# Softmax division moved behind the weighted sum, layer norm by tokens

## The reference, cut to what matters

```python
# branch A, 8 heads of 64: attention over the keys that an indexer selected
logits = where(selected, q @ k.T * HEAD_DIM**-0.5 + bias, NEG)
p = softmax(logits)                     # exp(l - max) / sum over the keys
attn = p @ v
# branch B, 512 channels: causal depthwise convolution c, then
c = (c - mean) * rsqrt(var + EPS) * g + b    # LayerNorm over the 512 channels
c = silu(c)
```

## Time and profile before

| | us |
|---|---|
| median of 3 runs (1861.46 to 1861.98) | 1861.76 |
| the profiled execution, its own time | 1863.46 |
| span of its trace | 1861.6 |
| PE busy in the span | 1763.3 |
| DVE busy | 1217.5 |
| ACT busy | 764.4 |
| POOL busy | 382.3 |

### The profile page before, as it was taken

How to read it: one execution, slowest core, us unless ns; L and a number is a source line. 1 busy time by engine, 2 the same in 40 slices (tenths; PEclk the granted TensorE clock), 3 DMA queues, 4 the chain that set the end, 5 groups by cost and what they waited for, 6 DMA issues and landing times.

```text
span 1861.6 us, 30230 instructions
## 1 busy us (share of the span) xinstructions
PE 1763.3 (95%) x11736; PEld 1587.2 (85%) x11736; DVE 1217.5 (65%) x2161; ACT 764.4 (41%) x1609; POOL 382.3 (21%) x457
## 2 busy tenths in 40 slices
PE   7978999999899987988999999999999999999999
PEld 6936999999889854667988789999999999888877
DVE  4279998999799666766453577555565654444443
ACT  4376666221565267655122443322222222333332
POOL 4104332331784122330000001111111112000000
PEclk9999999999999998998999999999999999999999
DMA  6411112221212424774332213222222222657574
GB/s 200 72 53 46 35 40 104 96 100 47 84 49 69 157 59 153 255 259 183 140 119 75 84 52 94 72 71 72 71 77 72 77 72 94 214 172 239 176 238 153
DMA packets 92881, 209.22 MB, mean 112 GB/s; under 512 B 13334, under 2 KB 32694, under 8 KB 92484
## 3 DMA queue, kind: packets, MB, share of 16 engines
q1 hardware_dynamic: 86555, 193.26, 32.4%
q10 hardware_dynamic: 6192, 14.16, 1.9%
HBM read 167.77 MB, written 39.58 MB: 111 GB/s over the span
## 4 chain that ended last, share of the span: by engine, by line
PE 40%; issue 14%; DVE 3%; ACT 2%; DMA 1%; POOL 1%; SPq 1%; POOLq 0%; DVEq 0%; ACTq 0%
PE ps L831 12%; PE ps L833 12%; PE ps L832 12%; DVE buf L1687 1%; DMA buf<-f_scr 1%; PE ps L1083 1%; PE ps L1060 1%; DVE buf L1893 1%; ACT buf L1493 1%; DVE buf L2259 1%; PE ps L1102 0%; PE ps L1117 0%; PE ps L1073 0%; SPq L799 0%; PE ps L1089 0%
## 5 line engine op out<-in xcount | busy, mean ns | idle before, releaser
L833 PE MATMUL ps<-buf,buf 128*128 128x288 f32 (+3 forms) x2660 | 877.3, 330 | 0.0
L832 PE MATMUL ps<-buf,buf 128*128 128x288 f32 (+3 forms) x2660 | 877.2, 330 | 0.0
L831 PE MATMUL ps<-buf,buf 128*128 128x288 f32 (+3 forms) x2484 | 828.5, 334 | 19.9 <-DVE buf L1687 10.7
L833 PEld LDWEIGHTS ps<-buf,buf 128*128 128x128 f32 (+1 forms) x2660 | 501.2, 188 | 24.4
L832 PEld LDWEIGHTS ps<-buf,buf 128*128 128x128 f32 (+1 forms) x2660 | 501.5, 189 | 23.5
L831 PEld LDWEIGHTS ps<-buf,buf 128*128 128x128 f32 (+1 forms) x2484 | 467.9, 188 | 48.7 <-DVE buf L1687 13.4
L1687 DVE TENSOR_TENSOR buf<-buf,buf 128x512 fp32r<-128x512 f32 (+6 forms) x359 | 317.3, 909 | 200.4 <-ACT buf L1678 123.4
L1841 DVE SCALAR_TENSOR_TENSOR buf<-buf,buf,buf 128x1024 f32<-128x1024 f32 x240 | 198.3, 867 | 4.0
L2410 POOL TENSOR_TENSOR buf<-buf,buf 128x288 f32<-128x288 f32 x88 | 78.9, 901 | 416.9 <-DVE buf L2129 375.3
L1780 DVE TENSOR_SCALAR_CACHE_REDUCE buf<-buf,buf 128x384 uint8<-128x384 f32 (+6 forms) x169 | 139.8, 887 | 1.2
L2305 POOL TENSOR_TENSOR buf<-buf,buf 128x256 fp32r<-128x256 f32 x96 | 89.8, 968 | 183.9 <-ACT buf L1313 183.9
(11 more groups left out here) (203 smaller groups left out, 1953.3 us busy)
## 6 DMA issues: line engine op xcount, KB each, us to landing
buf<-in_w_ffn SPq DMA_DIRECT2D x66, 512.0 KB, 3.7
buf<-in_w_ffn SPq DMA_DIRECT2D x88, 256.0 KB, 2.7
buf<-in_cache_k SPq DMA_DIRECT2D x16, 1024.0 KB, 7.4
buf<-in_cache_v SPq DMA_DIRECT2D x16, 1024.0 KB, 10.2
f_scr<-buf SPq DMA_DIRECT2D x22, 576.0 KB, 4.1
buf<-f_scr SPq DMA_DIRECT2D x66, 192.0 KB, 3.9
buf<-in_w_cols SPq DMA_DIRECT2D x24, 512.0 KB, 3.8
buf<-in_x SPq DMA_DIRECT2D x18, 512.0 KB, 4.2
```

What stands on the lines that cost most here:

```text
L831: mm(dst, whi, xhi, start=start, stop=False)
L832: mm(dst, whi, xlo, start=False, stop=False)
L833: return mm(dst, wlo, xhi, start=False, stop=stop)
```

## The change

The probabilities stay unscaled. DVE takes only the reciprocal of each unit's sum. After the second pair of every two, PE spreads the four columns of inverse sums into bank 7 beside the weighted sums, as four matmuls of the broadcast column with the identity. ACT copies them to SBUF (`rcrow`), and a step later DVE multiplies the two pairs' results, 128 by 128 each, in SBUF.

In the layer norm the squares become the stationary operand and one column of `ones` the moving one, so that the sums come out with tokens on partitions, one number each. ACT copies these 9 columns, POOL raises them to -1/2, PE spreads each token tile's column along partitions (`spread_rstd`, two tiles a step from step 8), and DVE multiplies a tile of all four channel groups at a time (`over_std`). `swish` moves from loops 10 to 13 to loops 13 to 16. Some semaphores are merged under one name, which changes no order.

```diff
@@ SP
-            sp.wait_ge(S("sqsum_done"), NG)
+            sp.wait_ge(S("sums_done"), 2 * NG)
@@ PE
-                    if c:
-                        pe.wait_ge(S("std_made"), c)
-                    else:
+                    if c == 0:
                         pe.wait_ge(S("d_made"), CT * NG)
-                for j in range(CT):
-                    l = mm(bank(6, G), ones, cT[:, j, tok(c, G)] if k == 0 else sqc[:, c % 2, j],
-                           start=j == 0, stop=j == CT - 1)
+                    for t in range(3):
+                        for j in range(CT):
+                            l = mm(bank(6)[:, 3 * c + t:3 * c + t + 1], sqc[:, c % 2, j, tok(t)], ones[:, 0:1],
+                                   start=j == 0, stop=j == CT - 1)
+                l.then_inc(S("sums_done"), 1)
+            def spread_rstd(t):
+                if t == 0:
+                    pe.wait_ge(S("rik_made"), 2)
+                if t >= 2:
+                    pe.wait_ge(S("dn_made"), t - t % 2)
+                mm(bank(6)[:, tok(1 + t % 2)], rsq[:, t:t + 1].to_broadcast([P, P]), ident).then_inc(S("rstd_spread"), 1)
...
-                    pe.wait_ge(S("p_made"), x + 1)
+                    pe.wait_ge(S("exp_done"), u + 1)
...
                             pe.wait_ge(S("attn_made"), attended_by[unit_step[u]])
+                            pe.wait_ge(S("rcrow_made"), attended_by[unit_step[u]] // 2)
...
+                if p >= 2:
+                    pe.wait_ge(S("rcrow_made"), p // 2)
...
+            def spread_sums(m):
+                pe.wait_ge(S("rc_made"), 4 * m + 4)
+                for n in range(4 * m, 4 * m + 4):
+                    l = mm(bank(7)[rows(n), tok(1 + n // 2 % 2)], rc[:, n % 8:n % 8 + 1].to_broadcast([P, HD]), ident)
+                l.then_inc(S("rc_spread"), 1)
...
                     weighted(i, step(i - 3, "prompt"))
+                    if step(i - 3, "prompt") % 2:
+                        spread_sums(step(i - 3, "prompt") // 2)
...
+                for t in range(2 * (i - 8), min(2 * (i - 8) + 2, NT)) if i >= 8 else ():
+                    spread_rstd(t)
@@ ACT
+            def variance():
+                act.wait_ge(S("sums_done"), 2 * NG)
+                ac(ssq[:, 0:NT], bank(6, NT), ACT.Copy).then_inc(S("var_made"), 1)
...
+                if p % 2:
+                    act.wait_ge(S("rc_spread"), p // 2 + 1)
                 ac(attnT[:, c, tok(b)], bank(7, P), ACT.Copy).then_inc(S("attn_made"), 1)
+            def inverse_rows(m):
+                if m >= 2:
+                    act.wait_ge(S("attn_scaled"), 2 * (m - 1))
+                ac(rcrow[m % 2], bank(7)[:, P:3 * P], ACT.Copy).then_inc(S("rcrow_made"), 1)
...
+                if i == 7:
+                    variance()
-                if 10 <= i < 10 + CT:
-                    swish(i - 10)
+                if 13 <= i < 13 + CT:
+                    swish(i - 13)
...
                     attended(step(i - 3, "prompt"))
+                    if step(i - 3, "prompt") % 2:
+                        inverse_rows(step(i - 3, "prompt") // 2)
...
-            act.wait_ge(S("attn_made"), N // 2)
+            act.wait_ge(S("attn_scaled"), N // 2)
@@ DVE
+            def over_std(t):
+                dve.wait_ge(S("rstd_spread"), min(t - t % 2 + 2, NT))
+                ve.tensor_tensor(cT[:, :, tok(t)], cT[:, :, tok(t)],
+                                 bank(6)[:, tok(1 + t % 2)].unsqueeze(1).to_broadcast([P, CT, P]), ALU.mult)\
+                    .then_inc(S("dn_made"), 1)
+            def inverse_sum(unit):
...
+                ve.reciprocal(rc[:, n % 8:n % 8 + 1], sm[:, n % 4:n % 4 + 1]).then_inc(S("rc_made"), 1)
+            def over_sums(m):
+                dve.wait_ge(S("rcrow_made"), m + 1)
+                for h, p in enumerate((2 * m, 2 * m + 1)):
+                    b, c = pairs[p]
+                    dve.wait_ge(S("attn_made"), p + 1)
+                    ve.tensor_tensor(attnT[:, c, tok(b)], attnT[:, c, tok(b)], rcrow[m % 2][:, tok(h)], ALU.mult)\
+                        .then_inc(S("attn_scaled"), 1)
...
-                    else:
-                        dve.wait_ge(S("dn_made"), CT)
...
+                if step(i - 4, "prompt") is not None and step(i - 4, "prompt") % 2:
+                    over_sums(step(i - 4, "prompt") // 2)
...
-                if 8 <= i < 10:
-                    for j in ((0, 1, 2), (3, 4, 5, 6))[i - 8]:
-                        over_std(j)
+                for t in range(2 * (i - 8), min(2 * (i - 8) + 2, NT)) if i >= 8 else ():
+                    over_std(t)
@@ POOL, at the head of its loop
+                if i == 8:
+                    pool.wait_ge(S("var_made"), 1)
+                    ch.link(gp.tensor_scalar(msq[:, 0:NT], ssq[:, 0:NT], 1.0 / CH, EPS, ALU.mult, ALU.add))
+                    gp.tensor_tensor(rsq[:, 0:NT], msq[:, 0:NT], mhalf[:, 0:NT], ALU.pow).then_inc(S("rik_made"), 1)
```

More of the change, by code:

```diff
@@ L278, in build @@
         cT = uT[:, :, 0:NTOK]
+        rcrow = [uT[:, j, NTOK:NTOK + 2 * P] for j in range(2)]
         NLOG = (PB - 2) * H
-        std = scoreS
         onehot = take(RN, o_w + CONVO + NTOK)
@@ L1027, in _ @@
             pe.wait_ge(S("vN_made"), NT)
-            pe.wait_ge(S("uo_made"), 2)
+            pe.wait_ge(S("state_made"), 4)
             def layer_sums(k, c):
@@ L1035, in layer_sums @@
                         pe.wait_ge(S("d_made"), CT * c)
+                    for j in range(CT):
+                        l = mm(bank(6, G), ones, cT[:, j, tok(c, G)], start=j == 0, stop=j == CT - 1)
                 else:
                     pe.wait_ge(S("sq_made"), c + 1)
-                    if c:
-                        pe.wait_ge(S("std_made"), c)
-                    else:
+                    if c == 0:
                         pe.wait_ge(S("d_made"), CT * NG)
-                for j in range(CT):
-                    l = mm(bank(6, G), ones, cT[:, j, tok(c, G)] if k == 0 else sqc[:, c % 2, j],
-                           start=j == 0, stop=j == CT - 1)
-                l.then_inc(S("csum_done" if k == 0 else "sqsum_done"), 1)
+                    for t in range(3):
+                        for j in range(CT):
+                            l = mm(bank(6)[:, 3 * c + t:3 * c + t + 1], sqc[:, c % 2, j, tok(t)], ones[:, 0:1],
[7 more added lines that the diff above has]
+                mm(bank(6)[:, tok(1 + t % 2)], rsq[:, t:t + 1].to_broadcast([P, P]), ident).then_inc(S("rstd_spread"), 1)
             def rows(h):
@@ L1110, in weighted_s @@
                     pe.wait_ge(S("attnS_made"), 2 * st_)
+                else:
+                    pe.wait_ge(S("dn_made"), NT)
                 for k in range(9):
@@ L1388, in _ @@
                 if t == NGLU + 1:
-                    act.wait_ge(S("u_turned"), 1)
-                    ac(uo, bank(6), ACT.Copy).then_inc(S("uo_made"), 1)
-                    ac(ut[0:HIST], bank(7)[0:HIST], ACT.Copy).then_inc(S("uo_made"), 1)
+                    act.wait_ge(S("state_turned"), 2)
+                    ac(uo, bank(6), ACT.Copy).then_inc(S("state_made"), 1)
+                    ac(ut[0:HIST], bank(7)[0:HIST], ACT.Copy).then_inc(S("state_made"), 1)
                 if t + 3 < NCOL:
@@ L1453, in _, with deviations @@
                 values(t)
[L1456 to L1461, removed]
-                else:
[L1463 to L1468, removed]
+            def deviations(c):
+                act.wait_ge(S("d_made"), CT * (c + 1))
+                if c >= 2:
+                    act.wait_ge(S("sums_done"), NG + c - 1)
+                ac(sqc[:, c % 2], cT[:, :, tok(c, G)], ACT.Square).then_inc(S("sq_made"), 1)
+            def variance():
+                act.wait_ge(S("sums_done"), 2 * NG)
+                ac(ssq[:, 0:NT], bank(6, NT), ACT.Copy).then_inc(S("var_made"), 1)
             def swish(j):
-                act.wait_ge(S("dn_made"), j + 1)
+                act.wait_ge(S("dn_made"), NT)
                 ac(cT[:, j], cT[:, j], ACT.Silu, scale=lng[:, j:j + 1], bias=lnb[:, j:j + 1])\
@@ L1511, in _ @@
             for i in range(len(steps) + 6):
-                if 5 <= i < 5 + NG:
-                    layer_norm(1, i - 5)
+                if i == 7:
+                    variance()
                 if i in (2, 3, 5):
-                    layer_norm(0, (2, 3, 5).index(i))
+                    deviations((2, 3, 5).index(i))
                 if step(i - 5, "sample") is not None:
                     outputs(step(i - 5, "sample"))
-                if 10 <= i < 10 + CT:
-                    swish(i - 10)
+                if 13 <= i < 13 + CT:
+                    swish(i - 13)
                 if second_unit(i - 2):
@@ L1871, in less_mean @@
             def less_mean(c):
[L1872 removed]
+                dve.wait_ge(S("sums_done"), c + 1)
                 for j in range(CT):
@@ L1875, in less_mean @@
                                             ALU.mult, ALU.add).then_inc(S("d_made"), 1)
[L1877 to L1885, removed]
```

(9 more changed lines are left out.)

17 lines of the change are left out of this document (8 added, 9 removed).

## The result

The changed kernel took 1865.77 us (median of 16 runs, 1860.85 to 1869.09), the kernel before beside it 1862.02 (16 runs): ratio 1.0017, 95% interval 1.0009 to 1.0025, 3.2 us slower. The forecast was 6 us faster; the time lies within its range, on the other side of no change. The profiled execution took 1868.29 us, with a span of 1866.5.

What follows compares the result with a forecast made beforehand. PE, busy 1763.3 of the 1861.6 us span, was taken as the bound, so only its gaps, half clock and added work counted; the terms summed to -6.0 us off the 1861.76 median, 1855.8 us, range 1847 to 1868.6 (forecast's own 1851 to 1859).

Steps and rivals of the forecast that it cites:

- Gap at 693.4: Before step 14, PE's 1.01 us wait for DVE goes as DVE's scaling of the probabilities is removed: -1.0 us.
- gaps from step 14: From step 14 to 850 us, freed DVE returns part of PE's 12 us of idle time and half clock: -7.0 us.
- Spreads: Sixteen spreadings of the inverse sums on PE, 0.44 us each, counted whole because PE is full there: +7.0 us.
- Copies: Sixteen ACT copies of the spread sums out of PSUM, 0.38 us each, partly delaying PE: +2.0 us, bounds 0 and 9.8.
- The stall: PE's 6.80 us wait before the first sample, during DVE's three reciprocals (7.73 us), goes: -6.8 us.
- Half clock behind it: PE's slow first sample logits and eight transposes after its wait before the first sample return to full clock: -2.6 us.
- Swish later: Same activations and table loads; PE's waits for ACT around them move into steps 13 to 16: 0, give or take 3.
- New products and their spreads: Layer norm, loops 8 to 12: nine DVE products of about 0.7 us, +1.0; nine spreading matmuls on PE, +2.0 us.
- Sums of squares: On PE, 24 records (8.4 us) go and 72 one-column records (7.8 us) come: -0.6 us, between -6.2 and +1.4.
- The end: Before the merge, PE's last spreading (0.44) and ACT's copy (0.38) delay the first weights' rounding: +1.2 us (0.8 to 2.5).
- ACT becomes what PE waits for: Rival, steps 14 to 40: copies and spreadings are exposed and late ACT cuts DVE's gain: +6.8, 1868.6 us; chance 0.18.
- The stall only moves: Rival, loops 8 to 12: the new layer norm products hold up the chain, adding 6.0: 1861.8 us, no change; chance 0.22.

Runs made afterwards that it cites:

- e5: Changed kernel's layer norm only, probabilities scaled on the pair as before, sums of squares streaming 56 columns of ones: 1860.23 us, ratio 0.9984 to the kernel before.
- e6: Changed kernel with 56-column sums of squares, inverse sums made but not spread, copied or multiplied (prompt's attention unscaled): 1854.97 us, ratio 0.9954 to the kernel before.
- e2: Kernel before with only the change's unscaled probabilities (inverse sums spread, copied, multiplied), layer norm as before: 1864.44 us, ratio 1.0011.
- e9: The kernel before, unchanged, profiled a second time: 1866.57 us, one execution.
- e4: Changed kernel with the four swishes in loops 13, 18, 23 and 28 instead of 13 to 16: 1862.85 us, ratio 1.0001 to the kernel before.
- e3: Changed kernel with the sums of squares streaming 56 columns of ones instead of one: 1861.77 us, ratio 0.9991 to the kernel before.
- e8: e5 with swish computed by tanh on ACT and the rest on DVE a loop later: 1873.27 us, ratio 1.0054 to the kernel before.
- e11: e8 with its four swishes in every second loop (13, 15, 17, 19): 1857.16 us, ratio 0.9969 to the kernel before.

## Why the prediction was wrong

Read against the forecast's steps, in its order:

- *Gap at 693.4 (-1.0)* and *gaps from step 14 (-7.0)*: -8 in all, -5.3 by e5 to e6, and not in the place that was forecast. Up to the first sample freeing DVE gave 3.0 us in A2 (e2 against before says 1.6: 35.4 to 33.8) where 1.0 was forecast, from step 14 on less than 2 where 7.0 was, from step 18 on 0.2. The waits view had said so: PE waited for ACT. The step that read "over half begin at a late DVE" out of one gap failed. That gap of 1.97 us and the half clock behind it stand in the first profile alone (D 115.4); in the three others (D 111.7 to 112.2) the gap is 0.58, and the nine transposes take 1.20 where they took 2.14. From e9:

```profile
813.64 1.09 PE L1083 MATMUL ps<-buf,buf 128*128 128x128 f32 x8 [0.58 <-ACT buf L1493]
...
815.85 1.20 PE L1089 MATMUL ps<-buf,buf 128*128 128x128 f32 x9
```

- *Spreads (+7.0)*: each took 0.54 from its start to the next row, 0.1 more than counted, and yet they cost 2.5 in all. In D half of their time went into what had been PE's idle time and slower clock. The step "count them whole" failed.
- *Copies (+2.0)*: with the 32 products (0.44 us each in place of the forecast's 0.3) and the end, +4.3. At the end PE's merge waits for L1526 and the rounding behind it, as forecast.
- *The stall (-6.8)*: right. No DVE row over 1.5 us is left there and no gap of PE over 3.
- *Half clock behind it (-2.6)* and *the gap of 1.16 (-1.2)*: right at their place. The first sample's logits take 2.14 us where they took 4.07, and the next logits begin without a gap. It doesn't show in B and C together, 46.1 before and 45.8 after in the means, because new rows stand there: five tiles' spreads of the layer norm (1.4 us) and three of the inverse sums (1.6), which are booked under +2.0 and +7.0.
- *Swish later (0, give or take 3)*: right within that. B loses 9.7 us and C gains 9.4, since the swishes with PE's waits for ACT and the low clock behind them went from B to C (clock 0.68 over 720 to 730 before, 0.70 over 740 to 750 after); e4 shows that their price goes where they go. What they cost in B before is not measured by itself.
- *New products and their spreads (+1.0, +2.0)*: 0.69 us for each product and about 0.14 for each of the spreads' 18 records; PE does not wait for the products, DVE waits 2.4 for L1053. In A2 e5 is 4.8 below before (30.6 to 35.4), the terms said -6.8 + 1.0 + 2.0 - 0.6 = -4.4.
- *Sums of squares (-0.6)*: **the step that failed.** As a row it was nearly right: 72 records took 8.8 us where 7.8 was forecast, +0.4 in place of -0.6. The Trainium skill, TensorE: Matmul & The Clock Gate, section LDWEIGHTS (loading the stationary operand), gives columns/1.2 ns for a load, so an estimated 107 ns for 128 columns: the trace comes near with 114 ns a record (2.74 us over 24), and is far from the 25 ns in that page's section Back-to-back issue gap. What the term left out was the clock behind these rows: 5.4 us in A2 (4.6 to 6.2 over after's four profiles), 4.0 us in the medians (e3). The forecast named a lower clock there as what would break it, and gave it neither a price nor a rival.
- *The end (+1.2)*: right: from the last sample's logits to the merge it was 30.5 to 30.9 us before and is 31.3 to 32.6.
- *Outside the stage (0)*: +1.2 of waits in the feed-forward stage, cause open, and about 1 that can't be told from chance.

In the four profiles of each kernel the stage is 1.6 us shorter where 6.0 was forecast. Without the 1.0 in front of the sums, about half of it chance, it is 0.7, and -6.0 with the sums' clock (+5.4) makes -0.6. That the errors of the other terms cancel is luck: the freed DVE, spreads and copies came out at +1.5 in sum, near their 2.2, by three errors. e3's stage is 5.7 us shorter than before's mean, as the forecast said, but that is one profile, at 1859.35 us one of the faster runs of e3, whose median is only 1.7 us (0.9991) below before, not clear of no change.

For the whole time the forecast's -6.0, the sums' clock by the medians (+4.0) and the 2.1 outside the stage make +0.1. The spans of the profiles say +0.5, the two sets of runs +3.2 and +1.5. What is left, 1 to 3 us, is not explained, and is about what such differences are good for.

Of the rivals, none came. "ACT becomes what PE waits for" was nearest: its place (730 to 746) and its sign are right, but PE's waits of `turn_p` for ACT's copy did not grow (6.3, and 6.6 before), and what ACT blocked there was swish. "The stall only moves" did not come: `over_std` delayed nobody (PE has no gap over 0.3 us between the first sample and the second), and what moved to the samples was the swish with its waits.

## What to carry to other kernels

A run of matmuls whose moving side is one column can cost more than its rows say: price the clock of what follows, and if the weight load sets the pace anyway, try streaming more columns. A gap and the half clock behind it are to be booked with the work that keeps PE waiting; if that work only moves, they move too. And where the waits view names one engine in a full stretch, freeing another may be worth little there, as DVE's 26 us from 730 to 850 were here, whatever share of it is busy. One profile is a thin ground for a gap's price: look whether the gap comes back in a second execution.

## What the runs showed of the hardware

In all four profiles of the changed kernel TensorE's granted clock fell to its lower level (1.2 GHz) for part of the time behind groups of 24 matmuls that streamed one column each, without a gap: its mean is 0.66 over 672 to 682, with PE busy for 9.89 of 10 us. With 56 columns in the same time it stayed at 1.00 (e3, PE busy for 9.80 of 10 us). The Trainium skill, TensorE: Matmul & The Clock Gate, section What's actually happening, says that the clock follows how busy PE has been; by the profile's busy time it did not follow it here.

Equal gaps are not followed by equal losses: behind the same 4.1 us of PE's gaps, 90 to 130 us after the merge begins, the clock over these 40 us is 0.96 in some executions and 0.91 in others, a loss of 1.6 or 3.6 us. The first and second profile of before:

```profile
955.11:995.11 40.00, 35.88 (x170) 31.15 (x170) 19.61 (x30) 11.44 (x19) 0.94 (x3) 0.96 0.23 79
956.23:996.23 40.00, 35.88 (x165) 30.92 (x164) 18.97 (x29) 11.44 (x19) 0.94 (x3) 0.91 0.22 79
```

Two more such places lie 180 to 280 us after the merge begins (1.00 or 0.97, and 0.97 or 0.93 over 50 us each, in before's four profiles). Together they put several us between executions of one kernel, more than most edits here are worth.

Tanh ran among exps with no table load between them (e8 and e11), as the Trainium skill, ScalarE: Activation LUTs, section Table sets: the hidden batching unit, says; Silu took a load on either side, 1.28 us each.
